# The down projections read their input rows from other start addresses in SBUF

## What is computed

```
def swiglu_ffn(h, w_gate, w_up, w_down):
    return (jax.nn.silu(h @ w_gate) * (h @ w_up)) @ w_down

def conv_ffn(h, w_up, conv_w, conv_b, w_down):
    a = causal_dwconv(h @ w_up, conv_w, conv_b)
    gate, val = jnp.split(a, 2, axis=-1)
    return (jax.nn.gelu(gate, approximate=True) * val) @ w_down
```

## The kernel before

| Moving rows | columns | from one row to the next | steps |
|---|---|---|---|
| `hid_hi`, `hid_lo`, and both `_b` | 256 | 1,024 bytes | 0 for all rows |
| `a1_hi`, `a1_lo` (shown as a_hi, a_lo, 256 columns) | 256 | 1,024 | 0 for all |
| `h_hi`, `h_lo`, `c_hi`, `c_lo` from column 16 | 256 | 1,088 | 64, 128, 192, 0 for k = 0 to 3 |
| `h_hi`, `h_lo` from column 14 | 258 | 1,088 | 56, 120, 184, 248 |
| `a_hi`, `a_lo` | 258 | 1,088 | 0, 64, 128, 192 |
| `pl_hi`, `m_hi` and their rests | 258 | 1,032 | grow by 8 from row to row |
| `h_hi`, `h_lo`, whole | 272 | 1,088 | 0, 64, 128, 192 |

## Time and profile before

### The profile page before, as it was taken

How to read it: one execution, slowest core, us unless ns; L and a number is a source line. 1 busy time by engine, 2 the same in 40 slices (tenths; PEclk the granted TensorE clock), 3 DMA queues, 4 the chain that set the end, 5 groups by cost and what they waited for, 6 DMA issues and landing times.

```text
span 2733.0 us, 53794 instructions
## 1 busy us (share of the span) xinstructions
PE 2627.5 (96%) x21278; PEld 2499.0 (91%) x21278; DVE 1708.0 (62%) x2393; ACT 1220.5 (45%) x1649; POOL 49.5 (2%) x98
## 2 busy tenths in 40 slices
PE   5799999899999999999899999999899999999997
PEld 1588887899999999999889899999899999999997
DVE  1388864586666666656755655555676666666667
ACT  1343454544444444445544454444554444444444
POOL 0000000000000000000000000000000000000000
PEclk9799999999999999999999999999999999999999
DMA  9988867476666666555444446566455555555554
GB/s 393 373 312 298 274 205 268 160 254 199 196 198 198 199 197 198 177 183 178 134 148 142 139 147 182 181 182 184 131 187 183 184 182 182 183 183 184 183 173 131
DMA packets 137088, 545.51 MB, mean 200 GB/s; under 512 B 15121, under 2 KB 17425, under 8 KB 124561
## 3 DMA queue, kind: packets, MB, share of 16 engines
q1 hardware_dynamic: 127312, 474.08, 53.8%
q0 software_dynamic: 9216, 67.11, 6.9%
q10 hardware_dynamic: 448, 2.75, 0.3%
HBM read 541.78 MB, written 2.10 MB: 199 GB/s over the span
## 4 chain that ended last, share of the span: by engine, by line
PE 89%; DVE 4%; ACT 3%; DMA 3%; issue 1%; ACTq 0%; DVEq 0%; SPq 0%
PE bank L1604 19%; PE bank L1605 19%; PE bank L1606 19%; PE bank L1741 9%; PE bank L1743 9%; PE bank L1742 9%; PE bank L1640 2%; DMA ada_pre<-in_ada_w 2%; DVE w_lo L992 1%; ACT w_hi L514 1%; PE bank L1681 1%; DVE y L1057 1%; ACT h_hi L590 1%; DMA bf<-in_f_bias 0%; PE bank L1699 0%
## 5 line engine op out<-in xcount | busy, mean ns | idle before, releaser
L992 DVE TENSOR_TENSOR w_lo<-raw,w_hi 128x1024 fp32r<-128x1024 f32 x836 | 1013.0, 1224 | 724.8 <-ACT w_hi L514 724.0
L514 ACT ACTIVATE w_hi<-raw 128x1024 fp32r<-128x1024 f32 x836 | 872.6, 1056 | 931.2 <-PE bank L1606 515.1
L1604 PE MATMUL bank<-h_hi,w_hi 128*128 128x258 f32 (+2 forms) x4112 | 1170.2, 285 | 29.1 <-DVE h_lo L1063 20.2
L1605 PE MATMUL bank<-h_lo,w_hi 128*128 128x258 f32 (+2 forms) x4112 | 1169.4, 284 | 0.0
L1606 PE MATMUL bank<-h_hi,w_lo 128*128 128x258 f32 (+2 forms) x4112 | 1165.5, 283 | 0.0
L1604 PEld LDWEIGHTS bank<-h_hi,w_hi 128*128 128x128 f32 x4112 | 777.1, 189 | 47.1 <-DVE h_lo L1063 21.6
L1606 PEld LDWEIGHTS bank<-h_hi,w_lo 128*128 128x128 f32 x4112 | 778.8, 189 | 0.0
L1605 PEld LDWEIGHTS bank<-h_lo,w_hi 128*128 128x128 f32 x4112 | 778.6, 189 | 0.1
L1741 PE MATMUL bank<-hid_hi,w_hi 128*128 128x256 f32 x1280 | 362.3, 283 | 0.0
L1743 PE MATMUL bank<-hid_hi,w_lo 128*128 128x256 f32 x1280 | 362.2, 283 | 0.0
L1742 PE MATMUL bank<-hid_lo,w_hi 128*128 128x256 f32 x1280 | 362.2, 283 | 0.0
(11 more groups left out here) (225 smaller groups left out, 2642.6 us busy)
## 6 DMA issues: line engine op xcount, KB each, us to landing
raw<-in_w_in SPq DMA_DIRECT2D x208, 512.0 KB, 4.1
raw<-in_w_ffn_up SPq DMA_DIRECT2D x176, 512.0 KB, 4.2
ada_raw<-in_ada_w POOLq DMA_DIRECT2D x64, 1024.0 KB, 7.1
raw<-in_w_gate SPq DMA_DIRECT2D x88, 512.0 KB, 4.1
raw<-in_w_up SPq DMA_DIRECT2D x88, 512.0 KB, 3.8
raw<-in_w_down SPq DMA_DIRECT2D x88, 512.0 KB, 4.2
raw<-in_w_ffn_down SPq DMA_DIRECT2D x88, 512.0 KB, 4.4
ada_pre<-in_ada_w SPq DMA_DIRECT2D x32, 1024.0 KB, 8.6
```

The source lines that it names most:

```text
L514: act.activation(w_hi[:, slot], raw[:, slot], ACT.Copy).then_inc(hi_ready, 1)
L992: dve.tensor_tensor(w_lo[:, slot], raw[:, slot], fp(w_hi[:, slot]), ALU.subtract).then_inc(lo_ready, 1)
L1604: pe.matmul(dst, wh, x_hi(kt), start=first and k == 0, stop=False)
L1605: pe.matmul(dst, wh, x_lo(kt), start=False, stop=False)
```

## The change

Each of the four tiles of a down projection (`hid_hi`, `hid_lo`, `hid_hi_b`, `hid_lo_b`) is replaced by four tiles of one row each, once for the first feed-forward part and once for the second. In the first part all rows begin at step 192. In the second they begin at steps 160, 176, 208 and 224 for k = 0 to 3. The hi and the lo row of the same k have the same step, since their bases (12288 and 16640, 0 and 4352) are multiples of 256. To make room, `tg`, `tu`, `us` and four tiles for sums of squares move on by 512 bytes, which leaves their steps as they were. No instruction, semaphore, size or order is changed on any engine; the instructions of the down projections and of the two that write their inputs only carry other addresses.

```diff
+HID_STEPS = ((192, 1216, 2240, 3264), (160, 1200, 2256, 3296))
...
-        hid_hi_b = place("hid_hi_b", "r3", 0, [128, 4, SEQ], f32r)
-        hid_lo_b = place("hid_lo_b", "r3", 4096, [128, 4, SEQ], f32r)
-        tg = place("tg", "r2", 20480, [128, 4, LIVE])
-        tu = place("tu", "r2", 24608, [128, 2, LIVE])
-        us = place("us", "r2", 20480, [128, 8, LIVE])
+        tg = place("tg", "r2", 20992, [128, 4, LIVE])
+        tu = place("tu", "r2", 25120, [128, 2, LIVE])
+        us = place("us", "r2", 20992, [128, 8, LIVE])
...
-        hid_hi = place("hid_hi", "r2", 12288, [128, 4, SEQ], f32r)
-        hid_lo = place("hid_lo", "r2", 16384, [128, 4, SEQ], f32r)
+
+        def hid_tiles(name, reg, first, steps):
+            return [place(f"{name}{t}", reg, first + step, [128, SEQ], f32r) for t, step in enumerate(steps)]
+
+        hid_parts = [[hid_tiles(f"hid_{name}_{part}", reg, first, HID_STEPS[part])
+                      for name, reg, first in (("hi", "r2", 12288), ("lo", "r2", 16640),
+                                               ("hi_b", "r3", 0), ("lo_b", "r3", 4352))] for part in range(2)]
...
-                    act.activation(hi[:, t + o], hid[:, t + o], ACT.Copy).then_inc(hid_hi_ready, 1)
+                    act.activation(hi[t + o][:, :], hid[:, t + o], ACT.Copy).then_inc(hid_hi_ready, 1)
...
-                    dve.tensor_tensor(lo[:, t + o], hid[:, t + o], fp(hi[:, t + o]), ALU.subtract)\
+                    dve.tensor_tensor(lo[t + o][:, :], hid[:, t + o], fp(hi[t + o][:, :]), ALU.subtract)\
...
-                        half_one(banks.bank() + j % 2, lambda kt: hi[:, kt], lambda kt: lo[:, kt], range(4),
+                        half_one(banks.bank() + j % 2, lambda kt: hi[kt][:, :], lambda kt: lo[kt][:, :], range(4),
```

More of the change, by code:

```diff
@@ L179, in build @@
         sq_pair = [place(f"sq_pair{n}", reg, off, [128, 2, 2, SUM_W[n]])
-                   for n, (reg, off) in enumerate((("r1", 0), ("r2", 26688), ("r2", 33920), ("r2", 28736)))]
+                   for n, (reg, off) in enumerate((("r1", 0), ("r2", 27200), ("r2", 33920), ("r2", 29248)))]
         sq_sum = [place(f"sq_sum{n}", reg, off, [128, 2, SUM_W[n]])
-                  for n, (reg, off) in enumerate((("r1", 4096), ("r2", 30784), ("r3", 32768), ("r2", 32832)))]
+                  for n, (reg, off) in enumerate((("r1", 4096), ("r2", 31296), ("r3", 32768), ("r2", 33344)))]
         sq = place("sq", "r2", 28672, [128, 2, SEQ])
         sq2 = place("sq2", "r3", 26624, [128, 2, LIVE])
-        hid_hi_b = place("hid_hi_b", "r3", 0, [128, 4, SEQ], f32r)
-        hid_lo_b = place("hid_lo_b", "r3", 4096, [128, 4, SEQ], f32r)
-        tg = place("tg", "r2", 20480, [128, 4, LIVE])
-        tu = place("tu", "r2", 24608, [128, 2, LIVE])
-        us = place("us", "r2", 20480, [128, 8, LIVE])
+        tg = place("tg", "r2", 20992, [128, 4, LIVE])
+        tu = place("tu", "r2", 25120, [128, 2, LIVE])
+        us = place("us", "r2", 20992, [128, 8, LIVE])
         sigg = place("sigg", "r2", 35328, [128, 2, SEQ])
@@ L749, in gate1, with up1 @@
                     act.activation(sg[:, t + o], tg[:, t + o, 2:], ACT.Silu, bias=tg[:, t + o, 0:1]).then_inc(gate_ready, 1)
[L751 removed]
+            def up1(i, b, t, hi=hid_parts[0][0]):
                 for o in range(2):
                     act.wait_ge(hid_ready, hids.next())
[L754 removed]
+                    act.activation(hi[t + o][:, :], hid[:, t + o], ACT.Copy).then_inc(hid_hi_ready, 1)
             def tap(dst, slot, i, b, t, first):
@@ L768, in gate2, with up2 @@
                     act.activation(sg[:, t + o], sg[:, t + o], ACT.Gelu_apprx_tanh).then_inc(gelu_ready, 1)
-            def up2(i, b, t, hi=hid_hi):
+            def up2(i, b, t, hi=hid_parts[1][0]):
                 tap(va, 4 + t, i, b, t, FT)
@@ L794, in ffn @@
                 chunk(10, gate)
-                chunk(10, up, hid_hi_b)
+                chunk(10, up, hid_parts[0 if with_ada else 1][2])
                 skip(8, 4)
@@ L1284, in scaled, with rest @@
                                          ALU.mult)
-            def rest(t, hi=hid_hi, lo=hid_lo):
+            def rest(t, hi, lo):
                 for o in range(2):
                     dve.wait_ge(hid_hi_ready, hids.next())
-                    dve.tensor_tensor(lo[:, t + o], hid[:, t + o], fp(hi[:, t + o]), ALU.subtract)\
+                    dve.tensor_tensor(lo[t + o][:, :], hid[:, t + o], fp(hi[t + o][:, :]), ALU.subtract)\
                        .then_inc(hid_lo_ready, 1)
@@ L1326, in up1 @@
                                              op0=ALU.add, op1=ALU.mult).then_inc(hid_ready, 1)
-                rest(t, *bufs)
+                rest(t, *(bufs or hid_parts[0][:2]))
             def more_taps(dst, slot, i, b, t, first):
@@ L1355, in up2 @@
                     dve.tensor_tensor(hid[:, t + o], va[:, t + o], sg[:, t + o], ALU.mult).then_inc(hid_ready, 1)
-                rest(t, *bufs)
+                rest(t, *(bufs or hid_parts[1][:2]))
             def ffn(gate, up, n_taps, n_gates, with_ada, step):
@@ L1384, in ffn @@
                 chunk(10, gate)
-                chunk(10, up, hid_hi_b, hid_lo_b)
+                chunk(10, up, *hid_parts[0 if with_ada else 1][2:])
                 down(n_zero)
@@ L1834, in chunk, with down @@
                         product(h_hi, h_lo, ST)
-                def down(hi=hid_hi, lo=hid_lo):
+                hids = hid_parts[0 if with_ada else 1]
+                def down(hi=hids[0], lo=hids[1]):
                     pe.wait_ge(hid_lo_ready, downs.next(4))
                     for j in range(8):
-                        half_one(banks.bank() + j % 2, lambda kt: hi[:, kt], lambda kt: lo[:, kt], range(4),
+                        half_one(banks.bank() + j % 2, lambda kt: hi[kt][:, :], lambda kt: lo[kt][:, :], range(4),
                                  True, True, banks.free())
@@ L1864, in ffn @@
                 down()
-                down(hid_hi_b, hid_lo_b)
+                down(hids[2], hids[3])
                 pair_sums(step + 1, (pair_squared, 8 * step + 16))
```

## The result

The changed kernel takes **2717.04 us** (median of 5 runs, 2715.51 to 2724.59) against 2735.04 us before (5 runs, 2733.84 to 2740.23). The ratio is 0.9937, with a 95% interval of 0.9921 to 0.9954: 18 us, or 0.6%, faster. The forecast was 2710.2 with a range of 2702 to 2721, so the time lies in the range, 7 us above the forecast. The profiled execution took 2717.04 us, its span is 2715.2 us.

What follows compares the result with a forecast made beforehand. The prediction took TensorE to bound the kernel. Gains of 14.1 us in the first part and 9.7 in the second, 23.8 in all, took 2734.0 to 2710.2 us, with a range of 2702 to 2721.

Steps and rivals of the forecast that it cites:

- What bounds the kernel: Whole kernel: TensorE, busy for 96% of the span; only a faster pace of 4,224 down projection matmuls shortens it.
- The first part: First feed-forward part, all rows at step 192: 120.0 falls to 113.3 ns on 2,112 matmuls, -14.1 us.
- Rival C: Down projections: 113.3 ns is not the settled pace; a long run falls back to 116.7, giving 2720 us; chance 0.08.
- The second part: Second feed-forward part, steps 160, 176, 208, 224: straight lines give 115.4 ns on average, -9.7 us on 2,112 matmuls.
- B: Second feed-forward part gains nothing, as rows touch 17 blocks of 64 bytes: 2717 to 2720 us; chance 0.15.
- The price of the 17th block: Second part's rows touching one more block of 64 bytes: 125.0 ns, read from 272 columns, so +10.6 us.
- the far end: Second part's worst bound: rows touching one more block of 64 bytes, 125.0 ns a matmul, +10.6 us.
- rival E: Slower kernel, from the extra block of 64 bytes in the second part: 2730.5 or 2737.6 us; chance 0.03.
- That the pace should differ by k: Changed profile, second feed-forward part: the matmul pace should differ by k; no size given for each k.
- The entry: Start of each of 22 down projections behind matmuls of another step: some 10 ns each, 0.1 us in a part.
- Rival A: Both feed-forward parts settle at 113.3 ns or better: 2706 us, or 2702 if the second is 2 ns below; chance 0.17.
- The two rules beside the rows: Skill pages: 16-byte SBUF lines imply no change; separate read ports and the issue gap imply about 109 ns a matmul.

Runs made afterwards that it cites:

- the map: Four kernels, each the changed one with four held steps: 2728.84, 2729.41, 2725.1 and 2729.96 us; the paces are tabled by step, with those known before.
- the last kernel but one above: Changed kernel with all down projection rows at step 0, weights moved on by 64 bytes, one foreign matmul ahead of each down projection: 2717.34 us.

## Why the prediction was right, and where it was not

- **What bounds the kernel: right.** 4,224 matmuls lost 17.3 us, and the span 17.8. Nothing came in their place: no gap of TensorE in the windows, DVE's and ACT's work unchanged.
- **The first part: right.** 113.3 ns was read from three matmuls of a half of c_hi and three of h_hi, as the pace towards which a block of six was moving. (In the c_hi block three starts come before those three, at 120, 110 and 120 ns, and not two.) It measured 113.4 in the mean of the long stretches, 13.9 us for 14.1. Rival C, that a longer run would fall back, did not come.
- **The second part: wrong, and this is the step that failed.** "As all four steps lie within 32 bytes of 192, I take straight lines" gave 115.4 ns and 9.7 us; it measured 118.4 and 3.4 us. These 6.3 us are nearly all of the 6.8 by which the time missed the forecast. The lines had no ground in the rows: no start between two multiples of 64 had been seen with 256 columns, and the low at 192 turned out to be one point, with 120.0 at 184 and 200. The points at the ends were of two kinds as well, 118 from six matmuls in passing and 120.0 from a held step.
- **That the time lies in the range** is owed to the rivals, above all to B with its 2717 to 2720 us and a chance of 0.15, up to which the range had been drawn, and not to the sum. B's 118.8 to 120.2 ns lie just above the 118.4 measured. It took them from rows with 258 columns, among them a_hi, which starts on multiples of 64, so they came near without saying why. The sign set for B, a pace over 118.8, was missed by 0.4 ns, although the second part lay much nearer to B than to the forecast. Its reason, a 17th block of 64 bytes touched, has no support from the map: 112 touches 17 and has 113.3, 128 touches 16 and has 118.6.
- **The price of the 17th block** was misread too. The 125.0 ns at 272 columns hold 16 columns more, which at one a cycle and 2.4 GHz are 6.7 ns; brought to 256 columns that is an estimated 118.3, so for the far end and for rival E the rows gave nothing above the 120.2 of a_hi.
- **That the pace should differ by k** in the second part: right, but slight. The means are 117.5, 118.4, 119.4 and 118.4 ns for k = 0 to 3.
- **The entry** was priced at 0.1 us for a part and taken for a passing matter. In the kernels at hand that was so. In general it was wrong: an entry can decide between 113.3 and 117.8 ns, or 113.3 and 118.7, for the 192 matmuls behind it.
- **Rival A** (113.3 in both) is what step 192 in both parts gives: 2706 was its price, 2707.3 its time.
- **The two rules beside the rows.** By the Trainium skill's "SBUF — State Buffer", section "Specifications (TRN2)", 64 lines of 16 bytes before and after would have meant no change; the runs show 6.7 ns between steps 0 and 192 held, with 64 lines each. By "TensorE: Matmul & The Clock Gate", section "Step-by-step: what each phase is for", the loading of weights takes nothing from the moving operand; moving only the weights by 64 bytes changed a_hi from 120.0 to 113.3. Here the measurements decide against both. The gap of about 262 cycles in "Back-to-back issue gap" should not have been set beside these rows as a rule for them: that section gives it for an isolated matmul and says that in a stream of weight loads and matmuls both set the spacing.

**What is shown and what is not.** Shown: the pace depends on how far the row starts from the weight blocks (modulo 256; the weights were moved by 64 bytes only), on the hi and the lo rows keeping the same distance, and on how the stream was entered. Not shown: the mechanism, for no run looked at SBUF itself, and what in an entry decides. Why 112 is low, and why moving the weights left the entry from 258 columns at 117.8, stays open; for 112 only one entry (from 144) was seen.

## What to carry to other kernels

Where TensorE is the bound and an f32 stream of 256 columns runs well above one column a cycle, try the start of the moving rows against the start of the weight blocks: here 192 bytes past them modulo 256 was worth 5.5% of each such matmul, 1.1% of the kernel, for a change of addresses alone. Measure each candidate step and don't interpolate: 8 bytes beside the best was as bad as the worst. Keep one step for the hi and the lo rows, and look at the pace behind every kind of entry.

## What the runs showed of the hardware that was not expected

- One layout has more than one settled pace. In one execution of the last kernel but one above, rows at the same distance from the weights ran at 113.3 ns in 20 down projections and at 117.8 in two; at step 16 it was 118.7 in nine and 113.3 in one; at 160, 117.3 in nine and 118.7 in one; at 128 past the moved weights, 118.7 in nine and 120.0 in one.
- Three paces came up in many down projections and repeat from half to half without a change: 113.3, 117.8 and 120.0 ns, that is 272, 282.7 and 288 cycles at 2.4 GHz for 256 columns. These are 16, 26.7 and 32 cycles above the 256 of the columns, or 48, 80 and 96 over the three matmuls of a set of terms.
- The low at 192 is gone 8 bytes to either side (184 and 200: 120.0 each), and there is a second one at 112.
